# Turning x and spreading the gate at the twelve sublayer boundaries: float32 matmuls replaced by TensorE transposes, with x scaled on VectorE first

## What is computed

```python
x = x + 0.5 * (1.0 + mod[:, 0, 2]) * swiglu(pre(x, 0), ffn_wi[l, 0], ffn_wo[l, 0])

def rmsnorm(x, g):
    xf = x.astype(jnp.float32)
    y = xf * lax.rsqrt(jnp.mean(xf * xf, axis=-1, keepdims=True) + EPS)
    return (y * g.astype(jnp.float32)).astype(x.dtype)

def pre(h, j):
    return rmsnorm(h, norm_g[l, j]) * (1.0 + mod[:, j, 1]) + mod[:, j, 0]
```

## Time and profile before

| | us |
|---|---|
| median of the three executions | 2624.07 |
| the three executions | 2619.49, 2625.35, 2624.07 |
| span of the profiled execution | 2623.9 |
| TensorE matmul busy | 2425.2 (92%) |
| TensorE weight load busy | 2043.9 (78%) |
| VectorE busy | 1732.2 (66%) |
| ScalarE busy | 1097.4 (42%) |
| mean granted TensorE clock | 0.947 |

### The profile page before, as it was taken

The page is one execution under the profiler, slowest core; times in us unless marked ns, Lnnn a source line. Parts: engine busy times, 40 slices in busy tenths (PEclk is TensorE's granted clock), DMA queues, the critical chain, the costliest instruction groups (busy, mean ns, idle before and its releaser), DMA issues.

```text
span 2623.9 us, 32924 instructions
## 1 busy us (share of the span) xinstructions
PE 2425.2 (92%) x11906; PEld 2043.9 (78%) x11906; DVE 1732.2 (66%) x2090; ACT 1097.4 (42%) x1220; POOL 0.2 (0%) x4
## 2 busy tenths in 40 slices
PE   8999994899999995999999898999999989899998
PEld 8788884788788773788788796778878878777886
DVE  4777576687587785677687644568757764455444
ACT  1443543434433454433534334544343333463443
POOL 0000000000000000000000000000000000000000
PEclk9999997999999995999999987999999998898999
DMA  9788440498588640498498832248858892324553
GB/s 336 253 302 274 152 137 8 138 319 265 193 296 293 217 164 29 147 314 271 164 320 294 228 117 85 97 160 301 275 193 282 294 277 94 113 81 129 176 185 111
DMA packets 349089, 530.28 MB, mean 202 GB/s; under 512 B 14833, under 2 KB 208465, under 8 KB 348881
## 3 DMA queue, kind: packets, MB, share of 16 engines
q1 hardware_dynamic: 349008, 529.18, 60.6%
HBM read 528.08 MB, written 1.05 MB: 202 GB/s over the span
## 4 chain that ended last, share of the span: by engine, by line
PE 78%; DVE 12%; ACT 5%; issue 2%; SPq 2%; DMA 1%; DVEq 0%; ACTq 0%
PE GU L1399 12%; PE GU L1403 12%; PE GU L1401 12%; PE PY L1399 9%; PE PY L1401 9%; PE PY L1403 8%; DVE wL L810 3%; ACT wH L496 2%; PE TM L1473 2%; PE PY L1417 2%; PE GU L1485 2%; DVE acc L839 1%; PE TM L1449 1%; PE PY L1729 1%; PE PY L1627 1%
## 5 line engine op out<-in xcount | busy, mean ns | idle before, releaser
L810 DVE TENSOR_TENSOR wL<-raw,wH 128x2048 fp32r<-128x2048 f32 x352 | 794.5, 2279 | 308.7 <-ACT wH L496 308.0
L496 ACT ACTIVATE wH<-raw 128x2048 fp32r<-128x2048 f32 x352 | 659.5, 1899 | 223.1 <-PE PY L1403 101.4
L1399 PE MATMUL GU<-wH,xH 128*128 128x512 f32 (+1 forms) x1600 | 634.4, 397 | 28.3 <-issue 11.6
L1403 PE MATMUL GU<-wH,xL 128*128 128x512 f32 (+1 forms) x1600 | 623.2, 390 | 0.0
L1401 PE MATMUL GU<-wL,xH 128*128 128x512 f32 (+1 forms) x1600 | 622.5, 389 | 0.0
L1399 PEld LDWEIGHTS GU<-wH,xH 128*128 128x128 f32 x1600 | 302.5, 189 | 93.6 <-issue 29.4
L554 ACT ACTIVATE hH<-TM 128x512 fp32r<-128x512 f32 x88 | 52.6, 598 | 747.1 <-PE TM L1449 747.1
L839 DVE SCALAR_TENSOR_TENSOR acc<-ada,cs,acc 128x512 f32<-128x512 f32 x448 | 336.9, 752 | 23.1 <-DVE acc L839 2.6
L1403 PEld LDWEIGHTS GU<-wH,xL 128*128 128x128 f32 x1600 | 301.9, 189 | 63.5
L1401 PEld LDWEIGHTS GU<-wL,xH 128*128 128x128 f32 x1600 | 302.5, 189 | 58.3
L1399 PE MATMUL PY<-wH,hH 128*128 128x512 f32 x704 | 226.7, 403 | 26.2 <-DVE hL L920 24.8
(11 more groups left out here) (295 smaller groups left out, 2324.5 us busy)
## 6 DMA issues: line engine op xcount, KB each, us to landing
ada<-in_ada_w SPq DMA_DIRECT2D x128, 1024.0 KB, 7.5
raw<-in_ffn_wi SPq DMA_DIRECT2D x176, 512.0 KB, 6.0
raw<-in_ffn_w_in SPq DMA_DIRECT2D x176, 512.0 KB, 5.6
raw<-in_ffn_wo SPq DMA_DIRECT2D x88, 512.0 KB, 4.4
raw<-in_ffn_w_out SPq DMA_DIRECT2D x88, 512.0 KB, 4.4
raw<-in_mix_w_in SPq DMA_DIRECT2D x64, 512.0 KB, 4.8
M<-in_ada_w SPq DMA_DIRECT2D x16, 1024.0 KB, 8.5
raw<-in_a_w_in SPq DMA_DIRECT2D x32, 512.0 KB, 4.7
```

What stands on the lines that cost most here:

```text
L496: act.activation(wH[:, slot, 0:words], raw[:, slot, 0:words], ACT.Copy).then_inc(s_high, 1)
L810: dve.tensor_tensor(wL[:, slot, 0:words], raw[:, slot, 0:words], wH[:, slot, 0:words], ALU.subtract).then_inc(s_split, 1)
L1399: pe.matmul(outs[i], aH, wh[i], start=first, stop=False)
L1403: ins = pe.matmul(outs[i], aL, wh[i], start=False, stop=last)
```

## The change

`gate_broadcast` and `turn_x` use `pe.transpose` against the identity. Since a transpose cannot scale, VectorE no longer scales the identity (one 128 x 128 instruction a tile) but x itself, into `xn`, in two halves of 128 x 512 a tile. TensorE waits for the first half before blocks 0 to 3 and for the second before blocks 4 to 7. `diag` is gone. Both happen in each of the 12 boundaries, for 2 tiles each.

```diff
@@ -149,7 +149,6 @@
-        diag = M[:, 2 * D:2 * D + NT * P].rearrange("p (t s) -> p t s", t=NT)
@@ -891,7 +890,10 @@
                     root(i)
-                    dve.tensor_scalar(diag[:, i, :], ident, rstd[:, i:i + 1], None, ALU.mult).then_inc(s_xn, 1)
+                    for h in range(2):
+                        half = slice(h * 512, (h + 1) * 512)
+                        dve.tensor_scalar(xn[:, i, half], x[:, i, half], rstd[:, i:i + 1], None, ALU.mult
+                                          ).then_inc(s_xn, 1)
                     if pieces and i == 0:
                         dve.wait_ge(s_eaten, t.next("done", pieces))
                         gated_output(1)
@@ -1406,15 +1408,15 @@
             def gate_broadcast():
                 pe.wait_ge(s_gcol, t.next(s_gcol))
                 for d in range(ND):
-                    ins = pe.matmul(TM[:, d // 4, (d % 4) * P:(d % 4 + 1) * P], shf[:, d * P:(d + 1) * P], ident,
-                                    start=True, stop=True)
+                    ins = pe.transpose(TM[:, d // 4, (d % 4) * P:(d % 4 + 1) * P], shf[:, d * P:(d + 1) * P], ident)
                 ins.then_inc(s_gp, 1)
 
             def turn_x(i):
 
-                pe.wait_ge(s_xn, t.next(s_xn))
                 for d in range(ND):
-                    ins = pe.matmul(PT[:, i, d, :], x[:, i, d * P:(d + 1) * P], diag[:, i, :], start=True, stop=True)
+                    if d % 4 == 0:
+                        pe.wait_ge(s_xn, t.next(s_xn))
+                    ins = pe.transpose(PT[:, i, d, :], xn[:, i, d * P:(d + 1) * P], ident)
                     if d % 4 == 3:
                         ins.then_inc(s_xt, 1)
```

## The result

| | before | after |
|---|---|---|
| median of the executions, us | 2624.71 | 2641.69 |
| lowest to highest | 2619.49 to 2626.13 | 2640.17 to 2643.43 |
| span of the profiled execution | 2623.9 | 2639.8 |
| mean granted clock | 0.947 | 0.939 |

The ratio is 1.0067, with a 95% interval from 1.0055 to 1.0078: the changed kernel is slower by 17 us, four executions of each. The profiled execution took 2641.59, and its span is 15.9 longer than that of before. The ratios further down are against executions of the kernel before that were timed beside each run (medians 2624.57 to 2625.40); two single executions, one of the kernel before (8321) and one of the kernel with the gate alone (10,688), are left out of them.

The account below looks back on a forecast made before the run. TensorE, holding 78% of the chain of waits, was taken to bound the kernel. Boundaries after feed-forwards 15.8, after mixers 5.4 and the first +2 gave +23 on 2623.9: 2647, likeliest case 2636 to 2656, eight in ten 2626 to 2656.

Parts of the forecast that it names:

- low end: The sum with the cheapest dips: 7 x 1.4, 4 x 0.6 and 0 at the first boundary, together +12 us.
- Dips after a feed-forward, 7 x 2.1: At seven boundaries after a feed-forward, a new stretch at the low clock costing 2.1 us each, between 1.4 and 3.0.
- The four after mixers, +5.4: At four boundaries after mixers, a dip of 2.1 replaces one of 0.9, plus 0.15 each: 5.4 us.
- The first boundary, +2: At the program's first boundary, less work before the first product lets the low clock reach into it: +2 us.
- The chain, +0.15 per boundary: Waits at each boundary: +0.43 before tile 0, -0.50 and +0.2 before tile 1, sum +0.15 us.
- The first half: Tile 0: VectorE's two halves of x delay L901 and the first product by 0.43 us; TensorE is no longer waited for.
- The second half: Tile 1: the turn takes 1.10 instead of 1.78, gaining 0.50 us, less some 0.2 of new waiting for xL.
- The gate: nothing: At each boundary the gate is 0.68 us shorter, but TensorE then waits for L894 anyway, so nothing is saved.
- A: Rival: no new dips at the boundaries, only the chain is left, 11 x 0.15 = 1.7, or 2626; chance 0.12.
- B: Rival: faster, a half of x scaled in under 0.3 us, tile 1 keeping its 0.50 per boundary, 2618; chance 0.08.
- C: Rival: each dip lasts 6.8 us and costs 3 at every boundary, +34, 2658; chance 0.04.
- The rule that was weighed: Skill's rule that transposes don't count for the clock as matmuls do: each boundary a 6 us gap, a dip certain.

Follow-up runs that it names:

- the gate alone: The kernel before with only the gate as transposes, the turn and VectorE unchanged: 2625.84, ratio 1.0005.
- the two filled kernels: The changed kernel with extra work on the identity in the idle times before and after the turn: float32 matmuls 2620.12, transposes 2621.46.
- the control: The kernel before with 7 extra float32 matmuls between gate and first turn, only at the four boundaries after mixers: 2622.88, ratio 0.9994.
- the filled kernel: The changed kernel with extra float32 matmuls of the identity in the idle times before and after the turn: 2620.12, ratio 0.9981.
- the second-tile kernel: The kernel before with x scaled on VectorE and turned by transposes for tile 1 only, tile 0 and gate unchanged: 2616.09, ratio 0.9971.

## Why the prediction was right, and where its sizes were off

The forecast was 2647, in a case that ran from 2636 to 2656; 2641.7 came. Its mechanism, a dip at every boundary, is shown by the clock record of the changed kernel and by the two filled kernels, in which the dips and the loss went together. The sum of +23 was 6 to 7 too high, with each of its four terms too large, so that no errors cancelled. (Its low end, 7 x 1.4, leaves out the 0.15 of the chain that the high end has; with it, that end is +13.) The terms compare as follows.

- **Dips after a feed-forward, 7 x 2.1 = 14.7.** All seven came. But six of them lasted 3.4 us and the boundaries with them grew by 1.2 to 1.4; only the one at 284.7 lasted 6.8, and it grew by 2.4. With the change's own -0.05 that makes the dips some 10.8. This is the term that was mis-sized most, by 4 us. The text had 1.6 for a short dip that begins with the first products, which is near what came, and 1.9 to 2.7 for one that begins in the gap, which is what the one at 279.5 cost. Its distinction held; what was off is that it took 2.1 for all, as if most began in the gap. Six of the seven began 0.5 us before the first product or later.
- **The four after mixers, +5.4.** They gained +2.7. The dips did grow, from 3.4 to 6.8 us. Set against the filled kernels, a dip there cost 0.65 to 1.3 us before (before less the control) and 1.2 to 2.1 now (after less the filled one), so 0.75 more on the mean where 1.2 was taken.
- **The first boundary, +2.** It grew by 1.66. Its weight loads show the reason that was given, transposes at the low clock and a first product that still runs at it (0.43 from 77.91 to 78.34):

```profile
74.77 1.57 PEld L1419 LDWEIGHTS PY<-cst,xn 128*128 128x128 f32 x8 [1.85 <-DVE xn L895]
77.74 0.28 PEld L1401 LDWEIGHTS GU<-wH,xH 128*128 128x128 f32 x1 [1.40 <-issue]
77.91 0.33 PEld L1403 LDWEIGHTS GU<-wL,xH 128*128 128x128 f32 x1
78.34 0.33 PEld L1405 LDWEIGHTS GU<-wH,xL 128*128 128x128 f32 x1
```

- **The chain, +0.15 per boundary.** It is -0.05 (the filled kernel against the control). The first half was right to two hundredths: the first product comes 6.16 after the gate instead of 5.71, which is +0.45 for an estimate of +0.43, and L903 doesn't wait for TensorE (but for the first boundary of the program). The second half was too dear: eight transposes take 0.83 to 1.0 from load to load (287.16 to 287.99 in the second-tile kernel) and not 1.10, which was scaled up from a single group of four in another place. From the second scale to tile 1 the gain was then 0.41, wait for xL included, instead of 0.3. That makes +0.04 up to tile 1. The other 0.1 lies in tile 1's first two weight loads: behind the wait for xL they follow each other after 0.11 (289.61 and 289.72), where without it they took 0.23 (290.92 and 291.15 in the kernel before).
- **The gate: nothing.** True by itself (1.0005). But the text costed the edit at nothing and then counted its missing work for the clock. With the turn changed too, the gate's transposes add 7.5 us, so the second is right and the first holds only for the chain. The expectation for the gate alone had it lose the clock as well, and that was wrong: the work that counts after a feed-forward stands behind the turn.

Of the rivals, A (no new dips, 2626) fell with the clock record, and its argument, that the longest single idle time of 2.3 us is hardly above the 1.82 of before, was near the truth (2.47) and did not help. B (faster) fell with its mechanism: a half of x takes 0.48, not under 0.3. Its effect, however, can be had: the second tile alone gives the 0.5 per boundary that B named. That the whole then took 2616, where B had 2618, is more than twelve times 0.5 gives; part of it, in the trace, is one dip fewer after a mixer. C (every dip 6.8 us, 2658) was the case at five of eleven boundaries.

The rule that was weighed would have made every dip certain whatever the idle times hold, as long as it is transposes. The Trainium skill, "TensorE: Matmul & The Clock Gate", Part 4: PE-mode transpose, says that they don't count for the clock as matmuls do. The gap filled by transposes kept 1.00 at eleven of eleven boundaries, the clock rose on transposes alone at the first, and the run took 2621.5, so for float32 transposes of 128 x 128 here the measurement says otherwise. The forecast came out right without that rule, and for another reason than it gives.

What stays open: why, with the same work in the gap, the clock falls 1.0 us before the first product at one boundary and 1.2 us after it at another, and exactly what amount of work, where in the gap, keeps the clock. The runs show which fillings held it and which did not, not the rule behind them.

## What to carry to other kernels

An edit that takes work from an engine that is waiting saves nothing there, and on TensorE it can cost: before shortening work in a gap between dense stretches, read the granted clock at that gap and at the others like it, and ask which of them has already lost it. Put a cheaper form of an operation only where other work of TensorE stands close around it (here the second tile's turn, some 8 us gained) and leave the longer form where it fills a gap. To find out whether a loss is clock or chain, fill the gap with work that has no effect and leave the waits alone: if the time comes back, it was the clock.

## What the runs showed of the hardware that I had not expected

- Transposes alone, in a gap of 6 us (7.5 after mixers), held the granted clock at 1.00 at all eleven boundaries between sublayers, and at the first one it rose from the low clock on nothing but transposes.
- The place of the work in the gap matters, not only its sum: 7 extra matmuls before the turn left dips at five of seven boundaries after a feed-forward (2633.6), 8 behind it left none there (2624.6).
- At the seven boundaries after a feed-forward the clock fell without any single idle time over 2.5 us (1.80 and 2.47 at the one at 279.5).
- Where TensorE was idle ahead of the first product, a dip that began 0.7 us or more before that product lasted 6.8 us (10 of 10), a later one 3.4 (18 of 18).
- A float32 transpose of 128 x 128 took 0.10 to 0.12 us from load to load at the full clock (eight in 0.83 at 287.16, eight in 0.99 at 276.90) and 0.20 at the low one (eight in 1.57 at 74.77).
